# The last token tile's row store on ScalarE's queue, the third expert's gate behind the router's products, final_g loaded early

## The reference, cut to what matters

```
hx2 = modulate(rms_norm(x, norm_ffn_g[l]), sh2, sc2)
x   = x + g2 * grouped_moe(hx2, router_w, router_b, w_exp_gate[l], w_exp_up[l], w_exp_down[l])
...
scores = sigmoid(h @ router_w);  the two best experts of the best group, weights w
for e in range(16):
    he  = silu(h @ w_gate[e]) * (h @ w_up[e])
    out = out + combine[..., e:e+1] * (he @ w_down[e])
...
return rms_norm(x, final_g)
```

## Time and profile before

| | us |
|---|---|
| median of 3 runs | 1619.79 (1618.65 to 1620.05) |
| the profiled execution | 1620.11 |
| its span | 1618.4 |
| busy: PE / DVE / ACT / POOL | 1540.6 / 682.5 / 314.3 / 38.5 |
| moved by DMA | 368.08 MB, mean 227 GB/s |

### The profile page before, as it was taken

One profiled execution on the slowest core, in us unless ns is written; L12 is line 12 of the kernel. 1 busy time (PEld: TensorE's weight loads), 2 busy tenths in 40 slices (PEclk: granted clock), 3 DMA queues, 4 the chain that ended last, 5 costly groups with the idle time before them and its releaser, 6 DMA issues. The chain is left out here.

```text
span 1618.4 us, 23021 instructions
## 1 busy us (share of the span) xinstructions
PE 1540.6 (95%) x9610; PEld 973.3 (60%) x9610; DVE 682.5 (42%) x1400; ACT 314.3 (19%) x721; POOL 38.5 (2%) x49
## 2 busy tenths in 40 slices
PE   5999989999999999999999999999999999899995
PEld 2774634654444445875546656786678888655553
DVE  1496765555755433361222116245533321611112
ACT  2121134321111100110011013234322211200001
POOL 0000000000000000000000021000000000000000
PEclk8999999999999999999999999999999999999998
DMA  9565411505433458469999986432115378799996
GB/s 367 194 234 182 131 39 53 131 27 182 135 140 112 161 182 317 203 230 394 414 391 392 402 347 233 132 104 66 39 40 170 117 260 311 295 426 429 420 410 284
DMA packets 127816, 368.08 MB, mean 227 GB/s; under 512 B 14237, under 2 KB 91319, under 8 KB 106972
## 3 DMA queue, kind: packets, MB, share of 16 engines
q1 hardware_dynamic: 118588, 344.86, 56.7%
q10 hardware_dynamic: 5392, 10.99, 2.3%
q0 software_dynamic: 3728, 10.71, 1.8%
HBM read 355.89 MB, written 12.98 MB: 228 GB/s over the span
## 5 line engine op out<-in xcount | busy, mean ns | idle before, releaser
L1304 PE MATMUL ps<-hT,ring 128*128 128x512 f32 (+1 forms) x768 | 260.3, 489 | 1.4 <-ACT arena L1774 1.4
L1177 PE MATMUL ps<-hT,ring 128*128 128x512 f32 (+1 forms) x544 | 211.8, 543 | 0.0
L1304 PEld LDWEIGHTS ps<-hT,ring 128*128 128x128 f32 x768 | 144.4, 190 | 108.1 <-issue 98.8
L1180 PE MATMUL ps<-ring,hT 128*128 128x256 f32 (+1 forms) x832 | 174.3, 366 | 7.1 <-DVE arena L2083 5.7
L1180 PEld LDWEIGHTS ps<-ring,hT 128*128 128x128 f32 x832 | 147.2, 191 | 37.0 <-issue 20.2
L1177 PEld LDWEIGHTS ps<-hT,ring 128*128 128x128 f32 x544 | 102.6, 194 | 97.3 <-issue 92.3
L1321 PE MATMUL ps<-arena,ring 128*128 128x512 f32 (+1 forms) x384 | 133.2, 487 | 0.0
L1467 PE MATMUL ps<-ring,arena 128*32 128x128 f32 (+2 forms) x1216 | 107.6, 343 | 3.5 <-DMA ring<-in_w_exp_gate 3.0
L1321 PEld LDWEIGHTS ps<-arena,ring 128*128 128x128 f32 x384 | 72.4, 190 | 50.6 <-issue 45.9
L1467 PE MATMUL ps<-arena 128*32 128x128 f32 (+1 forms) x1264 | 91.4, 328 | 0.7 <-DVE arena L2381 0.7
L1467 PEld LDWEIGHTS ps<-ring,arena 128*32 128x32 f32 (+2 forms) x1216 | 66.5, 129 | 42.2 <-issue 25.0
(11 more groups left out here) (288 smaller groups left out, 1561.2 us busy)
## 6 DMA issues: line engine op xcount, KB each, us to landing
ring<-in_w_in SPq DMA_DIRECT2D x54, 1024.0 KB, 6.2
ring<-in_w_ada SPq DMA_DIRECT2D x48, 1024.0 KB, 5.1
arena<-in_w_exp_down SPq DMA_DIRECT2D x18, 2048.0 KB, 19.1
arena<-in_w_exp_up SPq DMA_DIRECT2D x15, 2048.0 KB, 17.5
ring<-in_w_exp_down SPq DMA_DIRECT2D x14, 2048.0 KB, 17.2
ring<-in_w_exp_gate SPq DMA_DIRECT2D x12, 2048.0 KB, 17.8
ring<-in_w_exp_up SPq DMA_DIRECT2D x12, 2048.0 KB, 17.1
hT<-in_w_exp_gate SPq DMA_DIRECT2D x10, 2048.0 KB, 18.5
```

Of the source, the lines that this page charges most:

```text
L1177: last = pe.matmul(ps[:, bank, 0:tok.stop - tok.start], w[:, k, at:at + width], hT[:, k, tok], start=(k == 0), stop=(k == KD - 1))
L1180: last = pe.matmul(ps[:, bank, 0:width], hT[:, k, P * tok:P * (tok + 1)], w[:, k, at:at + width], start=(k == 0), stop=(k == KD - 1))
L1304: last = pe.matmul(ps[:, 0, lo:TOK], kview(n)[:, k, P * (m % 2):P * (m % 2 + 1)], hT[:, k, lo:TOK], start=(k == 0), stop=(k == KD - 1))
```

## The change

In the last layer only:
- SP issues the broadcast of `final_g` right behind down 0, ahead of the wait for `logits`. It goes to a region of its own, `region(5120, D)`. The three waits and the issue at the end are gone.
- SP issues gate 2 right behind the wait for `logits`.
- SP no longer stores the last row tile. ScalarE does, from its own queue: behind the sigmoid it waits for `h2_ready` and issues the same 512 KB store with the same semaphore `h2_out`.

Layer 0 issues what it issued, in the same order.

```diff
-        fg_row = ret_flat[:, 0:D]
+        fg_row = region(5120, D)
...
                 first_expert(2)
+                if l + 1 == DEPTH:
+                    sp.dma_start(fg_row, final_g.partition_broadcast(P)).then_inc(fg_in, 16)
                 sp.wait_ge(logits, 2 * before(nq, l + 1))
-                rows_out(NT - 1)
+                if RUN[l][2] < FIXED[l]:
+                    expert_tile(l, 2, 0, RUN[l][2])
+                if l + 1 < DEPTH:
+                    rows_out(NT - 1)
...
-                chosen = {2: expert_of(2)}
-                expert_tile(l, 2, 0, chosen[2])
-                if l == 0:
+                chosen = {}
+                if RUN[l][2] >= FIXED[l]:
+                    chosen[2] = expert_of(2)
+                    expert_tile(l, 2, 0, chosen[2])
                     expert_tile(l, 2, 1, chosen[2])
...
-            sp.wait_ge(x_mixed, 2 * before(nq, DEPTH))
-            sp.wait_ge(h2_ready, before(nq, DEPTH))
-            sp.wait_ge(moe.gate, EXPERTS * DEPTH - 2)
-            sp.dma_start(fg_row, final_g.partition_broadcast(P)).then_inc(fg_in, 16)
...
                 act.activation(score[:, 0:nq[l], :], score[:, 0:nq[l], :], ACT.Sigmoid).then_inc(scored, 1)
+                if l + 1 == DEPTH:
+                    act.wait_ge(h2_ready, before(nq, l + 1))
+                    act.dma_start(h_d[P * (NT - 1):P * NT, :], h_toks[l][:, NT - 1, :]).then_inc(h2_out, 16)
```

## The result

The change makes the kernel slower: a median of 1631.86 us (9 runs, 1628.62 to 1633.55) against 1620.93 us of the kernel before (9 runs, 1618.20 to 1625.72), a ratio of 1.0065 with a 95% interval of 1.0054 to 1.0076. That is 10.5 us, where 3.7 were forecast; the time lies above the stated range. The kernel before measures 1.1 us more in this comparison than the 1619.79 from which the forecast started. The profiled execution took 1631.47 us with a span of 1629.8.

What follows compares the result with a forecast made beforehand. From 1400 us the bound was one stream of loads at a fixed rate. TensorE's 7.2 us lag less 3.5 us of cover gave 3.7 us, added to 1619.8 for 1623.5 us; range 1616.3 to 1626.7.

Steps and rivals of the forecast that it cites:

- lag at gate 4: TensorE's lateness when it ends gate product 1 and gate 4 is issued: 4.7 us idle plus 2.5 us clock, 7.2 us.
- the cover: Queued DMA work ahead of gate 4 that absorbs TensorE's lateness: 3.5 us, with the remaining shift staying 3.7 us to the end.
- The bound: From 1400 us the last layer is one stream of bytes at a fixed rate, moved by bytes served earlier or starvation.
- the filled hole: 3.8 us of unused DMA engines at 1388 to 1393 us, filled by early gate 2; 2.5 us net of final_g.
- the late gather: Main case: gathered rows for experts 1 and 2 come late, making the kernel 3.7 us slower, 1623.5 us; chance 0.7.
- final_g early: Its bytes move from the end into the idle DMA stretch, taking 1.3 us of it; removal from the end gains nothing.
- The row store: Last row tile's store, issued at 1391.8 us with gate 2 in flight, lands at 1398.5 instead of 1394.7.
- The gather: Rows for experts 1 and 2, issued at 1399.4 us, take 9 us and leave TensorE idle for 4.7 us.
- The clock: After the idle wait TensorE's clock drops to 1.2 GHz for a stretch, costing 1.7 or 3.4 us; taken as 2.5.
- (a): Rival: the gather is in time, TensorE waits under 1.5 us, the stream keeps its 2.5 us: 1617.3 us; chance 0.13.
- (b): Rival: as (a), and down 14 near the end runs at 2.4 GHz, 3.5 us gained in all: 1616.3 us; chance 0.10.

Runs made afterwards that it cites:

- act_store_first: The kernel before, with the last row tile's store on ScalarE's queue and gate 2 held by SP until that store has landed; ratio 1.0008.
- store_behind_gate: The whole change, but the last row tile's store is issued by SP, behind gate 2 in its queue; measured twice, ratios 1.0027 and 1.0005.
- gate3_behind_gather: The whole change, but SP waits for the landing of the first gather before it issues gate 3; ratio 1.0021.
- g2_rows_early: The kernel before, with final_g and the six g2 row loads issued ahead of the wait for the logits, store and gate 2 as before; ratio 0.9998.
- final_g_late: The whole change without the early load of final_g, which is loaded at the end as before; ratio 1.0033.
- act_store_alone: The kernel before, with only the last row tile's store moved to ScalarE's queue, gate 2 and final_g not early; ratio 1.0057.
- gate3_a_little_later: The whole change, with 24 empty instructions on SP ahead of the issue of gate 3; ratio 1.0057.

## Why the prediction was right and wrong

The order of events was forecast rightly: a late store, a late gather, an idle TensorE, a lowered clock, a starved queue. Two terms of the sum failed. The gather was taken as 9 us and took 11.4, which made the lag at gate 4 9.6 us and not 7.2; and the cover was taken as 3.5 us and was 1.8. The wrong step in the second is "Later loads have more work ahead of them, so the shift stays 3.7". With the forecast cover, a lag of 9.6 would still have ended inside the range, 6.1 us above.

**The bound** was read rightly: one stream of loads from 1400 us on, whose end moves with what starves it. In the rows of the table from act_store_first down the end moves with gate 4, the load that starves it.

**Gate 2 early, the filled hole:** the 2.5 us were wrong, though in the late gather's sum they are given back and don't count. The hole was filled (share 0.82 for 0.68), but what could be issued ahead of gate 3 was then used up sooner, and idle time appeared right before gate 3 instead. In store_behind_gate, where the gather was in time, the share from 1398 to 1402 us is 0.27:

```profile
1398.00:1402.00 4.00, 3.52 (x34) 2.12 (x32) 3.55 (x14) 0.38 (x1) 1.06 (x1) 1.00 0.27 59
```

I had taken the queue in front of gate 3 as 3.2 us long, from an estimate of 6.6 us for 2 MB into an idle queue. The measured landing is 7.7 us (gate3_behind_gather), and in g2_rows_early gate 3 landed in 9.0. By these landings the hole was worth 9.8 - 9.0 = 0.8 us from the start, and by the bytes moved ahead of gate 3 0.7.

**final_g early:** nothing, as forecast, on its own; but in the whole change part of its 1.3 us ahead of gate 2 came out as lateness of the store (6.6 us for 5.9), and final_g_late shows how much hangs on them (a ratio of 1.0033 for 1.0065). I had counted them in the store's landing and not seen what they decide.

**The row store:** 6.7 us forecast (1391.8 to 1398.5), 6.6 measured. That the number is so near is partly luck, since the reason was incomplete. I laid it to gate 2 being in flight; act_store_alone shows that a second queue is as costly where the load is issued at the same moment. The rule of the Trainium skill ("DMA: Bandwidth & Descriptors", section "Queues, rings and completion order"), rings of their own served in turn on shared engines, agrees with act_store_alone: packet for packet with the load, 9.2 us, and 2.6 alone. In the change the store's first packet started 4.0 us after its issue, when the last 16 KB packets of gate 2 had started, and no run shows why it waited that long. What I had drawn from the section, that the store lands no earlier than gate 2, isn't what being served in turn means: in act_store_alone the store landed at 1404.9 us and gate 2 at 1405.2, in the change at 1402.0 and 1399.9.

**The gather:** the step that cost most. I took 9 us, between rows of 7.5 and 10.2. With its store late it has two outcomes beside gate 3, 5 and 11 to 13 us, by whether that 2 MB load is issued closer than some 0.8 us behind it; 9 lay between. TensorE waited 6.85 us, not 4.7.

**The clock:** 2.5 us forecast, 2.7 measured. Lag at gate 4: 7.2 us forecast, 9.6 measured.

**The cover:** 3.5 us forecast, 1.8 measured. For gate 4 itself the forecast was good: its second half landed 6.2 us later than before, 9.6 - 3.4. But "later loads have more work ahead of them, so the shift stays" was wrong. Counted from gate 3's issue, down 3 landed 8.3 us later and down 14 8.1. From its own issue down 3 took 11.6 us, where it had taken 12.9: the queue that had restarted empty had rebuilt all but 1.3 us of its backlog by then, so most of that backlog was no cover.

In sum 9.6 - 1.8 = 7.8 us against 7.2 - 3.5 = 3.7. The 1.8 is what is left of the lag at the end of the span, so this sum is a balance and no second proof of the 7.8. The medians are 10.9 us apart. The remaining 3 us are not settled: the store of the first row tile, ahead of which these kernels issue the same, goes out anywhere from 1380.4 to 1386.1 us in their profiles, and a gather behind gate 3 in the other executions (gate3_a_little_later, the same work, gives 9.9 us) would fill 2 us; neither is shown to be the cause.

**The rivals:** in the change none of them came. The gather in time, which (a) and (b) want, did occur in the profiles of final_g_late and store_behind_gate, but the gain that they forecast with it did not: the medians of the two are 5.3 and 4.4 us above before.

## What to carry to other kernels

In this kernel a short transfer that something waits for was safe in front of a large load in the same queue, and lost that safety in a queue of its own. Look for the packets of both: what counts is whose first packet moves first. Before an idle stretch of the DMA engines is counted as time to be won, ask what can be issued in the next one: if buffers hold the next load back, the idle time only moves. Where two landings differ by a race of issues, forecast the two outcomes with a chance for each, not a value between them.

## What the runs showed of the hardware

A gather of 128 rows of 4 KB took 4.6 to 5.0 us when issued into idle DMA engines 0.96 to 5.2 us ahead of a 2 MB load, and 11.4 to 12.8 us when issued 0.69 us ahead or later. Its first packet started 1.76 us after the issue into idle engines, a 2 MB load's 1.0 us, and a gather's 3.4 to 4.5 us when gate 3's packets had come first. Where 4 KB packets of a store or a gather and 16 KB packets of a load in another queue were under way together, about as many of one moved as of the other (128 and 128, 136 and 138). A 512 KB store took 2.6 us alone, 2.9 us in front of a 2 MB load in the same queue, and 9.2 us beside one issued 0.04 us after it in another queue. A 2 MB load into an idle queue landed in 7.7 us, though such loads land 5.0 us apart in a full one. 24 empty instructions on SP behind a wait shifted the next issue by nothing that can be seen (gate 3 still 0.2 us behind the end of gate product 0). TensorE kept its full clock (granted 1.00) over a wait of 9 us when it was given 40 small matmuls, and fell to 0.71 on average from 1416 to 1420 us when the 28 that it had ended 2.3 us early.
